# Down-projections whose shared products are summed in two buffers, with the other input sums parked in DRAM

## The reference, cut to what matters

```python
# first block, D_FF = 5632
z = rmsnorm(h, norm_ffn_g[l])
ff = (jax.nn.silu(z @ w_ffn_gate[l]) * (z @ w_ffn_up[l])) @ w_ffn_down[l]
h = h + ff.astype(h.dtype)
...
# second block, D_FF_2 = 8192
hm = rmsnorm_2(x, g_mlp[l])
x = x + jnp.square(jax.nn.relu(hm @ w_up[l])) @ w_down[l]
```

## Time and profile before

| what | value |
|---|---|
| median of 3 runs | 2530.38 us (2529.88 to 2530.49) |
| span of the profiled execution | 2528.4 us (its own time is not listed) |
| PE busy | 2509.3 us, 99% |
| PEld (weight loads of PE) busy | 2111.7 us, 84% |
| DVE busy | 1796.1 us, 71% |
| ACT busy | 1316.6 us, 52% |
| POOL busy | 409.8 us, 16% |
| moved by DMA | 478.31 MB, mean 189 GB/s |

### The profile page before, as it was taken

One profiled execution on the slowest core, in us unless ns is written; L12 is line 12 of the kernel. 1 busy time (PEld: TensorE's weight loads), 2 busy tenths in 40 slices (PEclk: granted clock), 3 DMA queues, 4 the chain that ended last, 5 costly groups with the idle time before them and its releaser, 6 DMA issues.

```text
span 2528.4 us, 32741 instructions
## 1 busy us (share of the span) xinstructions
PE 2509.3 (99%) x11904; PEld 2111.7 (84%) x11904; DVE 1796.1 (71%) x2081; ACT 1316.6 (52%) x1769; POOL 409.8 (16%) x287
## 2 busy tenths in 40 slices
PE   9999999999999999999999999999999999999998
PEld 7889888888888888888889988888888888888887
DVE  5556554555788988899656766565669788978874
ACT  5445454444555544555545554455556545654653
POOL 1001100112212211212002301031132211221110
PEclk9999999999999999999999999999999999999999
DMA  7645556575656556655656655465565565556564
GB/s 244 202 146 152 170 169 191 191 237 180 199 192 203 194 193 208 196 201 195 231 176 186 182 149 158 146 218 174 160 194 194 194 203 183 198 194 214 177 220 155
DMA packets 251124, 478.31 MB, mean 189 GB/s; under 512 B 15152, under 2 KB 38368, under 8 KB 249840
## 3 DMA queue, kind: packets, MB, share of 16 engines
q1 hardware_dynamic: 248416, 464.20, 57.5%
q0 software_dynamic: 2256, 12.13, 1.4%
q10 hardware_dynamic: 320, 0.20, 0.0%
HBM read 474.36 MB, written 2.12 MB: 188 GB/s over the span
## 4 chain that ended last, share of the span: by engine, by line
PE 94%; DVE 2%; issue 1%; ACT 1%; POOL 0%; DMA 0%; ACTq 0%; POOLq 0%; DVEq 0%
PE acc L1536 75%; PE acc L1562 6%; PE unit L1562 4%; PE unit L1590 3%; PE psO L1562 2%; PE psS L1562 2%; PE psO L1761 1%; ACT w_hi L1268 1%; PE psS L1656 0%; DVE w_lo L1883 0%; DVE x_sb L2080 0%; PE unit L1656 0%; ACT p L1410 0%; DVE stat L2117 0%; PE psS L1727 0%
## 5 line engine op out<-in xcount | busy, mean ns | idle before, releaser
L1883 DVE TENSOR_TENSOR w_lo<-w_raw,w_hi 128x1024 fp32r<-128x1024 f32 (+6 forms) x592 | 716.6, 1221 | 480.0 <-ACT w_hi L1268 474.8
L1268 ACT ACTIVATE w_hi<-w_raw 128x1024 fp32r<-128x1024 f32 (+6 forms) x592 | 596.1, 1017 | 462.0 <-PE acc L1536 439.4
L1536 PE MATMUL acc<-w_hi,xT_hi 128*128 128x512 f32 (+4 forms) x2020 | 783.4, 388 | 3.7 <-DVE xT_lo L1991 1.8
L1536 PE MATMUL acc<-w_lo,xT_hi 128*128 128x512 f32 (+4 forms) x2020 | 772.0, 382 | 0.0
L1536 PE MATMUL acc<-w_hi,xT_lo 128*128 128x512 f32 (+4 forms) x2020 | 771.5, 382 | 0.0
L1536 PEld LDWEIGHTS acc<-w_hi,xT_hi 128*128 128x128 f32 x2020 | 379.4, 188 | 73.7 <-issue 5.5
L1536 PEld LDWEIGHTS acc<-w_lo,xT_hi 128*128 128x128 f32 x2020 | 379.1, 188 | 70.0
L1536 PEld LDWEIGHTS acc<-w_hi,xT_lo 128*128 128x128 f32 x2020 | 379.6, 188 | 66.1 <-issue 0.5
L1914 DVE TENSOR_TENSOR w_lo<-w_raw,w_hi 128x1024 fp32r<-128x1024 f32 (+1 forms) x204 | 281.3, 1414 | 51.2 <-ACT w_hi L1292 49.2
L1536 PE MATMUL acc<-w_hi,hT_hi 128*128 128x512 f32 x720 | 281.2, 391 | 0.0
L1536 PE MATMUL acc<-w_lo,hT_hi 128*128 128x512 f32 x720 | 280.2, 389 | 0.0
(11 more groups left out here) (441 smaller groups left out, 3128.7 us busy)
## 6 DMA issues: line engine op xcount, KB each, us to landing
w_raw<-in_w_in SPq DMA_DIRECT2D x168, 512.0 KB, 3.6
w_raw<-in_w_down SPq DMA_DIRECT2D x104, 512.0 KB, 4.3
w_raw<-in_w_up SPq DMA_DIRECT2D x100, 512.0 KB, 4.1
w_raw<-in_w_ffn_down SPq DMA_DIRECT2D x76, 512.0 KB, 4.5
w_raw<-in_w_ffn_gate SPq DMA_DIRECT2D x68, 512.0 KB, 4.3
w_raw<-in_w_ffn_up SPq DMA_DIRECT2D x68, 512.0 KB, 3.9
w_raw<-in_w_out SPq DMA_DIRECT2D x64, 512.0 KB, 4.0
s_raw<-in_w_up SPq DMA_DIRECT2D x28, 512.0 KB, 6.0
```

Source lines behind the costliest of these rows:

```text
L1268: act.activation(w_hi[:, slot, 0:kc, 0:n], w_raw[:, slot, 0:kc, 0:n], ACT.Copy).then_inc(hi_split, 1)
L1536: ins = pe.matmul(ac[t][:, 0:n], a[:, l0 + c, t * P:(t + 1) * P], w[:, slot, c, 0:n], start=start and c == 0 and m == 0, stop=stop and c = ...
L1883: dve.tensor_tensor(w_lo[:, slot, 0:kc, 0:n], w_raw[:, slot, 0:kc, 0:n], w_hi[:, slot, 0:kc, 0:n].bitcast(F32), ALU.subtract).then_inc(lo_ ...
```

## The change

- In each half of a down-projection ACT now copies `psS` into a buffer of its own, `shared[:, 0]` (`p1_copied`). DVE adds that to the first output, and then sums the other shared banks in the two halves of `shared`, in place, as the banks' sums are needed: eight adds of 128x512, in parts of 2, 2, 3 and 1. `shared_read` is given in part 2 and not in part 3; a new semaphore `shared_added` follows the last add.
- The parts 2 and 3 of the first half stand behind the second and third tile of the second half.
- `shared` lies at 68 KB of the arena, over the upper part of `a_sum_lo` (66 to 72 KB). So POOL stores `a_sum_hi` and `a_sum_lo` in DRAM behind each `x_split` (two DMAs of 768 KB to `keep_sums`), and loads both again behind each of the three down-projections (`sums_back`, two DMAs of 768 KB), once `shared_added` is given. PE waits for `sums_back` ahead of the loop that follows.
- Other buffers move in the arena; waits are added where that makes two of them overlap (ACT's first `half` waits for `a_lo_split`, POOL's for `x_summed`, SP's fetch of a pair for `b_summed`, `h_sums` for `sums_kept`).
- Ground is laid for pairs whose raw weights land in the ring (`ring`) and for another home of the buffers (`FAR`); the values used are the old ones (three pairs per half, `NEAR`, no ring), so plans and matmuls stay as they were.

```diff
@@ schedule
-        one = block_pair(w, k0, 0, needs, turn, DOWN_PLANS[0], [both(x) for x in last])
-        i = [n for n, s in enumerate(one) if s[0] == "half"][0]
-        one = [("h_sums", 2 + turn)] + one[:i] + [("h_split",)] + one[i:]
-        return one + with_rest(0, block_pair(w, k0, 1024, (), turn, DOWN_PLANS[1]))
+        g = [group_of(DOWN, half, turn, 24) for half in range(2)]
+        one, rest = block_pair(w, k0, 24, 0, needs, turn, DOWN["plans"][0], g[0], [both(x) for x in last])
+        two, left_over = block_pair(w, k0, 24, 1024, (), turn, DOWN["plans"][1], g[1], [[x] for x in rest])
+        return with_sums(one, g[0], units) + two + left_over + [("sums_back",)] * more
@@ arena
-        a_sum_hi = arena("a_sum_hi", [P, 4, SEVENS, P], 98, F32R)
-        a_sum_lo = arena("a_sum_lo", [P, 4, SEVENS, P], 60, F32R)
+        a_sum_hi = arena("a_sum_hi", [P, 4, SEVENS, P], 60, F32R)
+        a_sum_lo = arena("a_sum_lo", [P, 4, SEVENS, P], 66, F32R)
+        shared = arena("shared", [P, 2, COLS], 68)
+        keep_sums = nc.dram_tensor("keep_sums", [2, P, 4 * SEVENS * P], F32, kind="Internal")
@@ SP, a pair
+                    if own:
+                        sp.wait_ge(lo_split, i - RING + 1)
+                        sp.wait_ge(b_summed, 2 * at["seven"])
@@ POOL
+                elif s[0] == "x_split":
+                    pool.wait_ge(a_lo_split, at["sums"] + 1)
+                    for i, v in enumerate((a_sum_hi, a_sum_lo)):
+                        pool.dma_start(keep_sums[i], v[:].bitcast(F32).rearrange("p j i q -> p (j i q)")).then_inc(sums_kept, 16)
                 elif s[0] == "h_sums":
...
+                    if group["home"] == NEAR:
+                        pool.wait_ge(sums_kept, 32 * at["kept"])
...
+                elif s[0] == "sums_back":
+                    pool.wait_ge(seven_done, at["seven"] + 1)
+                    pool.wait_ge(shared_added, at["group_added"])
+                    for i, v in enumerate((a_sum_hi, a_sum_lo)):
+                        pool.dma_start(v[:].bitcast(F32).rearrange("p j i q -> p (j i q)"), keep_sums[i]).then_inc(sums_back, 16)
@@ ACT
                     if h == 0:
                         act.wait_ge(seven_done, m + 1)
+                        act.wait_ge(a_lo_split, at["sums"])
...
+                elif s[0] == "shared" and s[2] == 0:
+                    to = HOME[s[3]["home"]]["shared"]
+                    act.wait_ge(seven_done, at["seven"] + 1)
+                    if at["added"]:
+                        act.wait_ge(shared_added, at["added"])
+                    act.activation(to[:, 0], psS[:].rearrange("p i k -> p (i k)"), ACT.Copy).then_inc(p1_copied, 1)
@@ PE, ahead of a loop
                     pe.wait_ge(a_lo_split, at["sums"])
+                    if at["back"]:
+                        pe.wait_ge(sums_back, 32 * at["back"])
@@ DVE, the parts
                     if part == 0:
-                        dve.wait_ge(seven_done, at["seven"] + 1)
+                        dve.wait_ge(p1_copied, at["group"])
+                        dve.tensor_tensor(x_(0, 0), x_(0, 0), to[:, 0], ALU.add)
+                        after(dve.tensor_tensor(to[:, 1], to[:, 0], p7, ALU.add))
+                    elif part == 1:
+                        dve.tensor_tensor(to[:, 0], to[:, 1], p6, ALU.add)
+                        after(dve.tensor_tensor(to[:, 1], to[:, 1], p5, ALU.add))
                     else:
                         for t in range(NT):
                             block_read(dve, at["block"] - 1, t)
-                    for b, t, src in (((0, 0, p1), (0, 1, p1), (1, 0, p1), (1, 1, p1)), ((0, 1, p7), (1, 0, p7), (1, 1, p7)),
-                                      ((0, 1, p6), (1, 0, p5), (1, 1, p6)), ((1, 1, p5),))[part]:
-                        ins = dve.tensor_tensor(x_(b, t), x_(b, t), src, ALU.add)
-                    if part == 3:
-                        ins.then_inc(shared_read, 1)
-                        dve.wait_ge(shared_read, at["seven"] // SEVENS + 1)
-                    else:
-                        after(ins)
+                        if part == 2:
+                            dve.tensor_tensor(x_(0, 1), x_(0, 1), to[:, 0], ALU.add)
+                            dve.tensor_tensor(to[:, 0], to[:, 0], p5, ALU.add).then_inc(shared_read, 1)
+                            after(dve.tensor_tensor(x_(1, 0), x_(1, 0), to[:, 1], ALU.add))
+                            dve.wait_ge(shared_read, at["group"] + 1)
+                        else:
+                            dve.tensor_tensor(x_(1, 1), x_(1, 1), to[:, 0], ALU.add).then_inc(shared_added, 1)
+                            dve.wait_ge(shared_added, at["added"] + 1)
```

More of the change, by code:

```diff
@@ L247, in block_steps, with block_pair @@
     return [("tile", b, k) for k in range(tiles_in(b))] + [("evac", b, (0, 1))]
[L250 to L256, removed]
+def block_pair(w, k0, kc, c0, needs, turn, plan, group, between=()):
+    b = [make_block(w, k0, kc, c0 + 512 * j, 512, "hT", 0, "add", c0 + 512 * j, needs, turn) for j in range(2)]
+    plain = [k for k in range(kc // CK) if not 1 <= k <= group["n"]]
+    k, q, out, part, between = [0, 0], 0, [], 0, [()] + list(between)
     for x in plan:
         if x == "S":
-            out.insert(-1, ("half", 0, q))
-            out.insert(-1, ("half", 1, q))
-            out.append(("seven", b[0], b[1], q))
+            i = max(n for n, y in enumerate(out) if y[0] == "tile")
+            out[i:i] = [("half", h, q, group) for h in range(2)]
+            out.append(("seven", b[0], b[1], q, group))
             q += 1
@@ L266, in block_pair @@
         k[j] += 1
-        out += turns.pop(0) if turns else ()
-        if q == SEVENS and part < 4:
-            out.append(("shared", c0, part))
+        out += between.pop(0) if between else ()
+        if q == group["n"] and part < 4:
+            out.append(("shared", c0, part, group))
             part += 1
@@ L272, in block_pair @@
             out.append(("evac", b[j], (0, 1)))
[L273 to L280, removed]
+    assert k == [len(plain)] * 2 and q == group["n"], (plan, k, q)
+    return out, [("shared", c0, p, group) for p in range(part, 4)]
 def both(name):
@@ L480, in number @@
 def number(steps):
-    out, shapes, wrote, seen, apart, sevenths = [], {}, {}, {}, set(), {}
-    c = dict(tile=0, lead=0, block=0, unit=0, split=0, hidden=0, seven=0, places=0, pairs=0, relus=0, silus=0, sums=0, squares=0, root=0, gained=0)
+    out, shapes, wrote, seen, apart, sevenths, held = [], {}, {}, {}, set(), {}, {}
+    c = dict(tile=0, lead=0, block=0, unit=0, split=0, hidden=0, seven=0, places=0, group=0, added=0, kept=0, back=0, after=2, relus=0, silus=0, sums=0, squares=0, root=0, gained=0)
     ahead = 0
@@ L510, in number @@
             c["sums"] += 1
+            c["kept"] += kind == "x_split"
         elif kind == "seven":
+            q, group = s[3], s[4]
+            own = q not in group["ring"]
+            assert own or c["tile"] % RING < RING - 1
             for h in range(2):
-                sevenths[c["tile"]] = (h, c["places"])
-                apart.add(c["tile"])
+                sevenths[c["tile"]] = (h, c["places"] if own else None, group["home"])
+                if own:
+                    apart.add(c["tile"])
+                else:
+                    at["summed", h] = held.get(c["tile"] - RING)
+                    held[c["tile"]] = 2 * (c["seven"] + 1)
                 c["tile"] += 1
@@ L517, in number @@
             c["seven"] += 1
-            c["places"] += 1
+            c["places"] += own
+            if q == group["n"] - 1:
+                c["group"] += 1
+                c["after"] = 0
+        elif kind == "half":
+            at["seven_tile"] = c["tile"] + 1
+        elif kind == "h_sums":
+            s[1]["clear"] = None if s[1]["home"] == NEAR else c["tile"]
+        elif kind == "shared":
+            at["added"] = c["added"]
+            c["added"] += s[2] == 3
+            if s[2] == 3:
+                for j in range(2):
+                    wrote["shared", s[1] // 512 + j] = c["added"]
+        elif kind == "sums_back":
+            at["group_added"] = c["added"]
+            c["back"] += 1
         elif kind == "x_sums":
@@ L560, in number @@
                 c["split"] += TRANSPOSES[s[1]][6] in ("split", "gain", "halves")
+            at["shared"] = c["group"] if c["after"] < 2 else None
+            c["after"] += 1
             c["unit"] += 1
@@ L575, in number @@
             c["places"] += len(OWN_PLACE) * n
-            c["pairs"] += n
+            c["group"] += n
+            c["after"] = 2
             c["relus"] += 4 * n if per == 4 else 0
```

184 lines of the change are left out of this document (122 added, 62 removed).

## The result

The changed kernel takes 2556.34 us (2555.59 to 2557.05, 4 runs); in the same session the kernel before took 2530.28 us (2529.88 to 2530.49, 4 runs). The ratio is 1.0103, 95% interval 1.0089 to 1.0118: slower by 26.1 us. The forecast was 2555.3 us.

A forecast was written before the change was run, and what follows sets the result against it. The prediction took PE, busy 2509.3 of 2528.4 us, as the bound. Stalls of +18.3 us and slow clock of +6.6 us gave 2553.3 us, plus 2.0 us from span to median: 2555.3 us, range 2543 to 2563 us.

The forecast's parts named there:

- What bounds the kernel: Whole kernel: PE is busy 2509.3 of 2528.4 us, so the time moves only by PE idle time removed or added.
- Fewer adds on DVE, copies on ACT: nothing: Down-projection halves: 18 adds fewer save 12 us of DVE, ACT gets one copy per half; both lie beside PE.
- When the last part is done: End of a down-projection: DVE's last shared add ends at 1000.5 us, and POOL sees it at about 1000.6.
- The stores: 0: Behind each x_split: two 768 KB stores of the sums cost 0, with a bound of 2 us each, twice.
- The reload: 8.0 us, stall 6.7 us, three times: Loop entries behind down-projections: both sums land after 8.0 us, PE idles 6.7 us each time, +18.3 us net.
- Rival 2: Loop entries: a quicker reload of about 5.8 us, stall 4.4 us, 2541.8 us if the clock stays up; chance 0.10.
- The clock: 2.2 us per stall: Behind each of three stalls PE runs at the 1.2 GHz level for a while, costing 2.2 us, +6.6 us.
- Rival 1: Loop entries: PE idles 6.7 us at each but goes on at 2.4 GHz, 2548.7 us; chance 0.26.
- The 1.84 us of before come back: Loop entries: PE's old waits for DVE of 0.66, 0.77 and 0.41 us lie inside the new stalls.

The follow-up runs named there:

- experiment 8: Changed kernel, but only the low sums loaded back and PE's wait moved behind the loop's first tile: 2538.36 us, 1.0034 of the kernel before.
- experiment 1: Changed kernel, but PE's wait for the reloaded sums moved ahead of the loop's first shared group: 2528.12 us, 0.9996 of the kernel before.
- experiment 4: Changed kernel, but only the low sums loaded back, PE's wait still at the loop's front: 2548.12 us, 1.0079 of the kernel before.
- experiment 5: Changed kernel, but the pair of sums loaded back twice in a row, PE waiting for all four: 2579.39 us, 1.0202 of the kernel before.
- experiment 3: Changed kernel plus thirty unread matmuls on PE ahead of each wait for the sums: 2550.54 us, 1.0086 of the kernel before.
- experiment 2: Changed kernel without the reload, later loops using the high sums in place of the low: 2531.38 us, 1.0008 of the kernel before.
- experiment 6: Kernel before, plus a POOL wait for shared_read ahead of loops behind a down-projection: 2527.49 us, 0.9992 of the kernel before.
- experiment 7: Changed kernel, only low sums stored and reloaded, PE's wait ahead of the loop's first shared group: 2527.69 us, 0.9992 of the kernel before.

## Why the prediction was right, step by step

- **What bounds the kernel.** Held. The span moved by PE's idle time and its slow spells: 29.3 us at the three entries, less the 1.84 us of before and some tenths, is 27.2 us; the span grew by 26.0. Most of the 1.2 us between the two is a wait of 1.1 us that the kernel before had elsewhere in its profiled run (PE for DVE's `memT_lo`) and the changed one had not; experiment 8, which has the change, shows it again, so it comes and goes between runs.
- **Fewer adds on DVE, copies on ACT: nothing.** Held, by the counts of instructions and by experiment 1, which has both and takes the time of before.
- **When the last part is done.** Said: added at 1000.5, POOL sees it at 1000.6. Measured: DVE's add of part 3 starts at 999.02 and ends at 999.7, POOL issues at 1000.26, PE was due at 1001.55. Against PE's due time the issue is 1.3 us ahead, 1.4 said. Two misses cancel in that: the add ends 1.85 us ahead of PE's due time, where 1.5 was said, and POOL's issue follows 0.56 us behind its end, where 0.1 was said. In the changed kernel the split was back at 1.23 us, as said:

```profile
997.87 1.23 DVE L1995 TENSOR_TENSOR w_lo<-w_raw,w_hi 128x1024 fp32r<-128x1024 f32 x1
999.02 0.68 DVE L2202 TENSOR_TENSOR x_sb<-x_sb,shared 128x512 f32<-128x512 f32 x1
```

- **The stores: 0.** Held; experiment 1 has them, and PE in the changed kernel has no new gap where they run.
- **The reload: 8.0 us, stall 6.7 us, three times.** Measured 8.3 us from the first issue to the second landing, stall 7.11, 7.19 and 7.03. It was scaled down by bytes from pairs of 1 MB beside the weights, and a transfer issued by POOL is not in proportion to bytes: experiment 4's 768 KB took 6.0 us and not half of 8.3. There was luck in it. The pair of the earlier trace rows with 9.9 us gives 7.4 in proportion; 8.0 came from leaning to the slower pair. An estimate on the line through 6.0 us (768 KB) and 8.3 us (1536 KB) gives 9.8 us for that pair's 2048 KB, so it is the scaling that was 0.9 us too short. The Trainium skill's fit (DMA: Bandwidth & Descriptors, Anatomy of one DMA), 2.0 us plus bytes at 436 GB/s, gives an estimated 5.6 us for the pair and 3.8 us for one; the runs show 8.3 and 6.0 beside the weights. The measurement decides. In experiment 5 the second pair, with PE idle and few weights to fetch (DMA share 0.80), landed 6.7 us behind its first issue (1009.07 to 1015.78). Rival 2 (5.8 us) is out; its ground was that SP fetches little while PE stands, and the DMA engines were busy to 0.98 until the landing.
- **The clock: 2.2 us per stall.** The mechanism held, the size was short: 2.5 to 2.8 us, 8.0 in all where 6.6 was said. With the stalls (21.3 for 20.1) the terms were 2.6 us too low. Only 1.0 us of that shows in the median (2556.34 for 2555.3), mainly because of the 1.2 us above, and that is luck. (The forecast's own range ends at 2564 us; stalls of 8 and slow spells of 2.8 us, its terms for that end, add up to 2561.) Rival 1 (2548.7 us) is out by the slow matmuls, and by experiment 3, which is that rival made real: 2550.54 us. This agrees with the Trainium skill (TensorE: Matmul & The Clock Gate, Part 1), by which idleness brings the low clock.
- **The 1.84 us of before come back.** They did, swallowed by the stall. The cause given (POOL's weight sums beside DVE's split) is shown by experiments 2 and 6. That it takes adds off DVE had no part in it.

What the sum left unsaid is that no part of the price was needed. The prediction noted that only the shared group behind three dense tiles reads the sums; experiment 1 shows that a wait there costs nothing that can be measured, with both sums just in time, and experiment 7 the same with 2 to 3 us to spare.

## What to carry to other kernels

Put a wait for data that is fetched again directly ahead of the instruction that reads it, not ahead of the loop: here three tiles (8.2 us) of independent work, with an issue 1.3 us ahead of them, just hid a landing of 9 us, and the wait's place alone was worth 27 us. Fetch back only what was overwritten: that made the margin 2 to 3 us. When a wait on an engine that is always busy is found, price two terms, the idle time itself and the slow spell of the clock behind it, and size the landing from transfers of the same queue, near the same size and beside the same traffic in the trace. Where a short wait on DVE comes and goes, look at what POOL does at that moment, before taking work off DVE.

## What the runs showed of the hardware

- **PE's clock falls in mid-kernel after short idle times, and not always after the same.** It fell in idle times of 2.45, 2.93, about 7 and about 14 us, and in or right behind those of about 5, and did not with 1.81 us nor after the 0.7 us of before. In the changed kernel the granted clock dropped 5.2, 2.6 and 2.1 us behind the end of the last matmul at the three entries, and at experiment 4's second entry 0.5 us behind PE's restart. Behind it the matmuls were 0.427 us apart and not 0.227, which cost 1.5 to 2.9 us each time, no more after 14 us of idleness than after 3.
- **DVE stands while POOL reads SBUF.** An instruction of DVE with two inputs in SBUF that starts during POOL's sum of weights ends about its own length behind POOL's end: 0.68 us became 2.30, 1.22 became 2.55, 2.70 and (experiment 2, third entry) 3.31. With POOL's end at 998.08, 1000.14, 1002.69 and 2344.21, less DVE's start, plus its own length, one gets 2.42, 2.68, 2.84 and 3.44 us, each about 0.13 us too long. The Trainium skill (SBUF — State Buffer, Who interferes with whom) has this as a lock: the instruction that comes second is blocked until the first ends; these rows agree, and not with two engines that share a rate. The other order shows the same from POOL's side. In the changed kernel DVE's split comes first and is not slowed, and POOL's sum (2.36 us in experiment 5, where DVE stands) takes 2.98:

```profile
1000.94 1.22 DVE L1995 TENSOR_TENSOR w_lo<-w_raw,w_hi 128x1024 fp32r<-128x1024 f32 x1
```

  The split ends at 1002.16, 0.77 us behind POOL's start at 1001.39; 0.77 and 2.36 make 3.13 us, 0.15 too long.
- **A reload was slower where PE worked beside it.** With PE idle `a_sum_lo`, second of its pair, landed after 7.68, 7.75 and 7.81 us in the changed kernel and after 7.60, 7.84 and 7.80 in the first pairs of experiment 5. With PE at work it took 8.97, 7.83 and 8.94 us in experiment 1 and 8.78, 8.74 and 8.12 in experiment 3, whose only edit is PE's thirty matmuls. The DMA engines moved 371 to 376 GB/s in the changed kernel and in experiments 1 and 3 alike, so it was not that they stood still. By what way PE's work reaches the transfer, no run here shows.
